# A two-block transformer kernel on one core: short attention pairs, the second down product, the end and the opening in another order

## The reference

```python
# first block: x += mixer(rms_norm(x)); x += conv_ffn(rms_norm(x))
z = h @ w_in                             # pool, q (16 heads of 64), k/v, gates, merge gates
p_c = masked_softmax(q @ k_cmp)          # over compressed keys
imp = sum over heads and overlap of p_c  # importance of each block of 64 keys
_, idx = top_k(imp + forced, 8)          # which 8 blocks each query may see
p_s = masked_softmax(q @ k_sel)          # selected blocks
p_w = masked_softmax(q @ k_win)          # window of 512
o = g0 * p_c @ v_c + g1 * p_s @ v_s + g2 * p_w @ v_w
# second block: x += hybrid_mixer(rmsnorm(x)); x += sqrelu_mlp(rmsnorm(x))
y = square(relu(rmsnorm(x) @ w1)) @ w2   # width 4096; "@ w2" is the second down product
return rmsnorm(x + y)                    # the end
```

## Time and profile before

| what | us |
| --- | --- |
| median of the runs | 2964.59 |
| profiled execution | 2968.41 |
| its span, first to last instruction | 2966.6 |
| TensorE busy | 2901.7 |
| VectorE busy | 2032.5 |
| ScalarE busy | 1447.7 |
| GpSimd busy | 466.8 |

### The profile page before, as it was taken

The page is one execution under the profiler, slowest core; times in us unless marked ns, Lnnn a source line. Parts: engine busy times, 40 slices in busy tenths (PEclk is TensorE's granted clock), DMA queues, the critical chain, the costliest instruction groups (busy, mean ns, idle before and its releaser), DMA issues.

```text
span 2966.6 us, 42764 instructions
## 1 busy us (share of the span) xinstructions
PE 2901.7 (98%) x16282; PEld 2407.7 (81%) x16282; DVE 2032.5 (69%) x3369; ACT 1447.7 (49%) x2448; POOL 466.8 (16%) x764
## 2 busy tenths in 40 slices
PE   9999999899999999999999999999999999999998
PEld 6888888778998887888888888777888788878886
DVE  6653246766775348999989952375655877778888
ACT  4552125887776125445544431275742544444445
POOL 0110004765554120000000000262012000000000
PEclk9999997999999999999999999999999999999999
DMA  4222231000000511333334323001102244474422
GB/s 151 73 84 71 82 117 44 2 1 2 2 2 1 200 56 64 114 114 114 109 133 178 121 86 125 29 2 36 43 29 72 100 166 161 161 302 148 155 100 86
DMA packets 89017, 269.50 MB, mean 91 GB/s; under 512 B 10496, under 2 KB 13696, under 8 KB 88432
## 3 DMA queue, kind: packets, MB, share of 16 engines
q1 hardware_dynamic: 77840, 226.63, 21.5%
q0 software_dynamic: 10976, 40.15, 3.9%
HBM read 190.73 MB, written 70.25 MB: 88 GB/s over the span
## 4 chain that ended last, share of the span: by engine, by line
PE 88%; DVE 4%; ACT 4%; issue 2%; DMA 1%; POOL 0%; SPq 0%; ACTq 0%; DVEq 0%; POOLq 0%
PE PS L256 31%; PE PS L3243 23%; PE PS L3265 15%; PE PS L919 3%; PE PS L933 3%; PE PS L905 2%; PE PS L904 2%; PE PS L1563 1%; PE PS L1598 1%; PE PS L1585 1%; PE PS L956 1%; ACT P_SHORT L1003 1%; PE PS L280 1%; ACT PT L1013 1%; PE PS L947 1%
## 5 line engine op out<-in xcount | busy, mean ns | idle before, releaser
L228 DVE TENSOR_TENSOR WLO<-RAW,WHI 128x1024 fp32r<-128x1024 f32 x94 | 115.7, 1231 | 361.4 <-ACT WHI L223 360.7
L223 ACT CAST WHI<-RAW 128x1024 fp32r<-128x1024 f32 x94 | 98.4, 1048 | 531.2 <-PE PS L256 511.1
L256 PE MATMUL PS<-HLO,WHI 128*128 128x512 f32 x992 | 306.4, 390 | 0.0
L3265 PE MATMUL PS<-DXH,PWH 128*128 128x512 f32 x656 | 256.2, 391 | 3.7 <-DVE DXL L2618 3.7
L3265 PE MATMUL PS<-DXH,PWL 128*128 128x512 f32 x656 | 255.9, 390 | 0.0
L3265 PE MATMUL PS<-DXL,PWH 128*128 128x512 f32 x656 | 255.7, 390 | 0.0
L3243 PE MATMUL PS<-XSH_T,PWH 128*128 128x512 f32 x596 | 233.1, 391 | 5.3 <-DVE PWL L2394 2.4
L3243 PE MATMUL PS<-XSL_T,PWH 128*128 128x512 f32 x596 | 231.9, 389 | 0.0
L3243 PE MATMUL PS<-XSH_T,PWL 128*128 128x512 f32 x596 | 231.9, 389 | 0.0
L256 PEld LDWEIGHTS PS<-HLO,WHI 128*128 128x128 f32 x992 | 186.8, 188 | 39.2
L3243 PE MATMUL PS<-XSH_B,PWL 128*128 128x512 f32 x456 | 177.4, 389 | 0.0
(11 more groups left out here) (444 smaller groups left out, 7160.4 us busy)
## 6 DMA issues: line engine op xcount, KB each, us to landing
W<-in_w SPq DMA_DIRECT2D x61, 1024.0 KB, 6.4
RAW<-in_w SPq DMA_DIRECT2D x96, 512.0 KB, 3.3
hidden<-W SPq DMA_DIRECT2D x54, 512.0 KB, 2.7
DXR<-hidden_t SPq DMA_DIRECT2D x24, 1024.0 KB, 5.3
DXR<-hidden SPq DMA_DIRECT2D x18, 1024.0 KB, 5.1
hidden_t<-W SPq DMA_DIRECT2D x32, 512.0 KB, 3.9
hidden_t<-T SPq DMA_DIRECT2D x16, 512.0 KB, 3.1
X<-in_x SPq DMA_DIRECT2D x8, 512.0 KB, 8.2
```

Of the source, the lines that this page charges most:

```text
L223: nc.scalar.copy(WHI[:, slot, :], RAW[:, slot, :]).then_inc(w_hi, 1)
L228: nc.vector.tensor_tensor(WLO[:, slot, :], RAW[:, slot, :], WHI[:, slot, :].bitcast(F32), ALU.subtract).then_inc(w_lo, 1)
L256: last = nc.tensor.matmul(o[:, half], w[:, slot, cols], x(k)[:, half], start=(k == 0 and w is WHI and x is hi), stop=(done and k == kcs - ...
L3265: last = nc.tensor.matmul(DOWN_BANK(i, p), wt[:, cols], xt[:, k, :], start=(opens and k == 0 and wt is d.pwh(n) and xt is d.xh[r]), stop=( ...
```

## The change

Six places, nothing in what is computed:

- Opening: unit 0 does its last two steps before unit 1 does. VectorE casts the third weight tile and takes its low part before it waits for the reciprocal root; ScalarE leaves that tile out.
- Short pairs, TensorE: up to pair 29, branch 0 of the second head ahead is scored before turn 2, branch 1 after the turns.
- Short pairs, ScalarE: where a pair has more than two turns (pairs 16 to 31), the first exponential of `ahead` comes before copy 2.
- Short pairs, VectorE: all four shifts and the first reciprocal of `ahead` come before CSUM, CMIN and the selection.
- Second down product: the last pair's sums are made beside factor 4 of group 0 instead of factor 0, and SP stores them after block 8 instead of before block 4.
- End: the first mean comes after product 0 and uses bank 0, which product (1, 0) then waits to have read; roots, squares, sums and scalings are in another order.

```diff
--- before.py
+++ after.py
@@ -299,12 +299,14 @@
             for k in range(lead, KC):
                 step(k, 1)
             return
-        for k in range(lead, KC):
-            if k == 6:
-                pe.wait_ge(consts[1], ALL_REST)
-                pe_mean(pe, n)
+        for k in range(lead, KC - 2):
             step(k, 0)
             step(k, 1)
+        pe.wait_ge(consts[1], ALL_REST)
+        pe_mean(pe, n)
+        for b in range(2):
+            for k in range(KC - 2, KC):
+                step(k, b)
 
     def narrow_product(pe, u, hi, lo):
 
@@ -402,7 +404,9 @@
         return N_GATE if i == 2 else P
 
     def act_z1_step(act, u):
-        if u < U_MIX:
+        if 0 < u < U_MIX:
+            if u == 1:
+                act.wait_ge(w_hi, 3)
             act_split(act, u + 2)
         v = u - 1
         if v in ROPE:
@@ -480,8 +484,6 @@
         if U_POOL < u <= U_Q:
             dve.wait_ge(pooled_done, u)
         dve_scaled(dve, 0, u, dst)
-        if u == 0:
-            dve_split(dve, 2)
         if u < U_Q:
             dve_window_sums(dve, u)
         if U_POOL <= u - 1 < U_Q:
@@ -888,11 +890,11 @@
 
         return m + 1 == PAIRS_SHORT
 
-    def pe_scores(pe, n):
+    def pe_scores(pe, n, branches=(0, 1)):
 
         s, qt, g, j = where(n)
         pe.wait_ge(q_lo, s + 1)
-        for branch in range(2):
+        for branch in branches:
             if not short(n):
                 pe.wait_ge(shifted, 2 * n - 1 + branch)
             elif n >= 2:
@@ -985,9 +987,14 @@
             if m in SCORED:
                 pe_cmp_scores(pe, SCORED[m])
             b = batches_of(m)
+            between = ahead and m < PAIRS_SHORT and not waits_for_all(m)
             for i in b[0]:
+                if between and i == 2:
+                    pe_scores(pe, 2 * ahead + 1, (0,))
                 pe_turn(pe, m, i)
-            if ahead and not waits_for_all(m):
+            if between:
+                pe_scores(pe, 2 * ahead + 1, (1,) if len(b[0]) > 2 else (0, 1))
+            elif ahead and not waits_for_all(m):
                 pe_scores(pe, 2 * ahead + 1)
             pe_use(pe, m, b[0])
             if ahead and waits_for_all(m):
@@ -1061,9 +1068,11 @@
             if m >= PAIRS_SHORT:
                 act_out_hi(act, m - 1)
             for i in b[0]:
+                if ahead and len(b) == 1 and i == 2:
+                    act_exp(act, 2 * ahead, 0)
                 act_copy(act, m, i)
             if ahead:
-                if len(b) == 1:
+                if len(b) == 1 and len(b[0]) <= 2:
                     act_exp(act, 2 * ahead, 0)
                 act_exp(act, 2 * ahead, 1)
             if 0 < m < PAIRS_SHORT:
@@ -1231,6 +1240,10 @@
             if ahead:
                 dve_shift(dve, 2 * ahead, 0)
                 dve_shift(dve, 2 * ahead, 1)
+                if m < PAIRS_SHORT:
+                    dve_shift(dve, 2 * ahead + 1, 0)
+                    dve_shift(dve, 2 * ahead + 1, 1)
+                    dve_inverse(dve, 2 * ahead)
             if m >= PAIRS_SHORT:
                 dve_out_lo(dve, m - 1)
             if m in SUMMED:
@@ -1241,7 +1254,7 @@
                 dve_select(dve, SELECTED[m])
             if m >= PAIRS_SHORT and next_seg(m, 1):
                 dve_queries_lo(dve, next_seg(m, 1))
-            if ahead:
+            if ahead and m >= PAIRS_SHORT:
                 dve_shift(dve, 2 * ahead + 1, 0)
                 dve_inverse(dve, 2 * ahead)
                 dve_shift(dve, 2 * ahead + 1, 1)
@@ -2758,13 +2771,13 @@
                     act_end_square(act, m)
                 if (i, p) == (6, 0):
                     break
-        for n in (11, 12, 13):
+        for n in (11, 12):
             act_end_square(act, n)
         act_end_root(act, 0)
-        for n in (14, 15, 16, 17):
+        for n in (13, 14, 15):
             act_end_square(act, n)
         act_end_root(act, 1)
-        for n in (18, 19):
+        for n in (16, 17, 18, 19):
             act_end_square(act, n)
         act_end_root(act, 2)
 
@@ -2918,11 +2931,12 @@
         sp.wait_ge(pw_lo, S2.prods + 4)
         for p in range(4):
             sp_w4(sp, D2, 1, p)
-        sp.wait_ge(t_sums, T_SUMS0 + 4 * FF2_PAIRS)
-        for b in range(2):
-            sp.dma_start(hidden_t[Q_LAST2, b], TSUM[b][:, :]).then_inc(D2.t_out, 16)
         for b in range(4, D2.blocks):
             sp_block(sp, D2, b)
+            if b == 8:
+                sp.wait_ge(t_sums, T_SUMS0 + 4 * FF2_PAIRS)
+                for i in range(2):
+                    sp.dma_start(hidden_t[Q_LAST2, i], TSUM[i][:, :]).then_inc(D2.t_out, 16)
             if b in (10, 17):
                 g = b // 7 + 1
                 sp.wait_ge(pw_lo, S2.prods + 28 * (g - 1))
@@ -2947,7 +2961,7 @@
     END_SQ0, END_SUM0, END_MEAN0, END_ROOT0, END_RSTD0 = 32, 32, 4, 4, 4
     end_prod, end_z, end_quad = job_done, hhi_done, evacuated
     END_PROD0, END_QUAD0, END_Z0 = jobs_before(U_FF2), jobs_before(U_FF2), SPLITS_BEFORE[3] + N_XS
-    END_BANK = (4, 5, 6)
+    END_BANK = (0, 5, 6)
 
     def quad_at(i, p, g=DOWN2_GROUPS - 1):
 
@@ -3025,24 +3039,25 @@
         dve_end_sum(dve, 8)
         dve_end_quad(dve, 0, 1)
         dve_end_sum(dve, 9)
+        dve_end_sum(dve, 10)
         dve_end_quad(dve, 0, 2)
-        dve_end_sum(dve, 10)
-        dve_end_sum(dve, 11)
-        dve_end_quad(dve, 0, 3)
-        dve_end_sum(dve, 12)
         dve_end_ready(dve, 0)
         dve_end_scale(dve, 0, range(0, 1))
+        dve_end_quad(dve, 0, 3)
+        dve_end_sum(dve, 11)
+        dve_end_sum(dve, 12)
+        dve_end_scale(dve, 0, range(1, 3))
         dve_end_quad(dve, 1, 0)
-        dve_end_scale(dve, 0, range(1, 3))
+        dve_end_scale(dve, 0, range(3, 5))
+        dve_end_quad(dve, 1, 1)
+        dve_end_scale(dve, 0, range(5, 6))
         dve_end_sum(dve, 13)
-        dve_end_quad(dve, 1, 1)
-        dve_end_scale(dve, 0, range(3, 5))
+        dve_end_quad(dve, 1, 2)
         dve_end_sum(dve, 14)
-        dve_end_quad(dve, 1, 2)
-        dve_end_scale(dve, 0, range(5, 6))
+        dve_end_scale(dve, 0, range(6, 7))
+        dve_end_quad(dve, 1, 3)
         dve_end_sum(dve, 15)
-        dve_end_quad(dve, 1, 3)
-        dve_end_scale(dve, 0, range(6, KC))
+        dve_end_scale(dve, 0, range(7, KC))
         dve_end_ready(dve, 1)
         dve_end_scale(dve, 1, range(KC))
         dve_end_ready(dve, 2)
@@ -3053,7 +3068,10 @@
         out = bank(END_BANK[i])[:, 0:cols.stop - cols.start]
         pe.wait_ge(end_sum, END_SUM0 + END_SUMMED_IN[i])
         pe.wait_ge(end_sq, END_SQ0 + (8, 16, 20)[i])
-        pe.wait_ge(end_quad, END_QUAD0 + i + 1)
+        if i:
+            pe.wait_ge(end_quad, END_QUAD0 + i + 1)
+        else:
+            pe.wait_ge(D2.quads, quad_at(5, 0))
         last = nc.tensor.matmul(out, ONES[:, :], END_SUM[:, cols], start=True, stop=(i == 0))
         if i:
             last = nc.tensor.matmul(out, ONES[:, :], SQ_LAST[:, cols], start=False, stop=True)
@@ -3066,6 +3084,8 @@
         pe.wait_ge(pw_lo, D2.prod0 + n + 1)
         if b:
             pe.wait_ge(D2.quads, quad_at(5, p))
+            if p == 0:
+                pe.wait_ge(end_root, END_ROOT0 + 1)
         else:
             pe.wait_ge(end_z, END_Z0 + p + 1)
             pe.wait_ge(D2.quads, quad_at(4, p))
@@ -3083,7 +3103,7 @@
         for b in range(2):
             for p in range(4):
                 pe_end_product(pe, b, p)
-                if p == 1:
+                if p == 0:
                     pe_end_mean(pe, b)
         pe_end_mean(pe, 2)
 
@@ -3206,7 +3226,7 @@
                 dve_block_lo(dve, D2, b, p)
             for made in D2.ws_of(g, i, p):
                 dve_dws(dve, D2, *made)
-            if g == 0 and i == 0 and p:
+            if g == 0 and i == 4 and p:
                 dve_t_sums(dve, Q_LAST2, p)
             if (g, i) == (DOWN2_GROUPS - 1, 5):
                 dve_end_z(dve, p)
@@ -3387,6 +3407,10 @@
         for rows in (slice(0, 32), slice(64, 96)):
             last = nc.vector.tensor_scalar(SIN[rows, :], SIN[rows, :], -1.0, None, ALU.mult)
         seq(dve, last)
+        dve.wait_ge(w_loaded[0], 32)
+        dve.wait_ge(job_done, 1)
+        nc.vector.tensor_copy(WHI[:, 0, :], RAW[:, 0, :]).then_inc(w_hi, 1)
+        dve_split(dve, 2)
         dve.wait_ge(rstd_done, 1)
         for u in range(U_POOL, U_MIX):
             dve_z1_step(dve, u)
```

## The result

The changed kernel takes 2971.14 us (median of 20 runs, 2968.11 to 2974.39), the kernel before 2964.88 (20 runs, 2961.39 to 2968.75): ratio 1.0019, 95% interval 1.0013 to 1.0025. It is 6.3 us slower. The forecast was 2962.4 with a range from 2952 to 2971.0, so it was wrong: in sign, and 0.14 us outside the range.

The account below looks back on a forecast made before the run. TensorE is busy 98% of the span, so gains come only where it stands still or runs at its lower clock. Terms: -3.6 - 3.2 - 2.9 + 7.5 = -2.2 us, giving 2962.4 us; range 2952 to 2971.

Parts of the forecast that it names:

- Opening, -3.6: Before the third tile's first product: TensorE restarts 1.92 us sooner and 1.7 of lower clock goes; 3.6 us gained.
- Second down product, -3.2: At its start: the low part comes 1.56 us sooner and 1.6 of work lost to the clock returns; 3.2 gained.
- End, -2.9: Last means and scalings: piece 2 follows piece 1 without a gap and begins 3 us sooner; gain 2.9 us.
- Pair 1, +1.0: Short attention: the sum moves behind ScalarE's exponential, so GpSimd's gated probabilities come 1.0 us later; cost 1.0.
- Pair 31, +3.3: Step to the long pairs: ScalarE's exponential ahead of two copies delays the sum and first long turn; cost 3.3 us.
- Pairs 16 to 30: Short attention: cost 1.0 us at pair 20, against a 1.2 us credit for scores filling waits before turns 2.
- 1.0 here and by the same walk at 8, 1.4 at 4: Pairs 12, 8, 4: selection waits for exponentials, then low parts, so the next pair's first shift is late; these costs in us.
- upper bound of 12: Attention's net cost at most 12 us, with every listed cost half as large again and no credit.
- two signs of being wrong: Wait before the first long turn no longer than before, or pairs 16 to 30 shorter by more than 3 us.
- Rival 1: The attention gains, between -6 and 0 us, as waits before turns go; total 2949 to 2955; chance 0.28.
- Rival 2: Pair 1's longer stall delays the return to full clock by 20 us, losing 8.7 us; total 2971; chance 0.13.
- Rival 3: Opening and down product: stalls shorten but the clock still drops, giving 1.9 + 1.6 only; total 2965.7; chance 0.10.

Follow-up runs that it names:

- k4: Changed kernel with the first head's reciprocal back behind sum, minimum or selection in the short pairs, the four shifts staying ahead: 2958.86 us, 0.9981.
- k5: Changed kernel with VectorE's old order in the short pairs, TensorE's and ScalarE's new order kept: 2954.51 us, 0.9961.
- k10: Changed kernel with the first head's reciprocal back behind sum, minimum or selection and pair 31 old on VectorE and ScalarE: 2954.62 us, 0.9964.
- k2: Kernel before with only the new order of the short attention pairs: 2978.92 us, 1.0051.
- k12: Kernel before with only the end in the new order: 2962.71 us, 0.9991.
- k8: Kernel before with only the last hidden pair's sums and their stores moved in the second down product: 2962.76 us, 0.9991.
- k14: Changed kernel with the first head's reciprocal back behind the selection, only in pairs with a selection (1, 4, 8, ... 28): 2961.53 us, 0.9986.
- k15: Changed kernel with the first head's reciprocal back behind the sum, only in pairs with a sum (1, 3, 7, ... 31): 2969.98 us, 1.0015.
- k3: Changed kernel with pair 31 alone in the old order on VectorE and ScalarE: 2968.64 us, 1.0009.
- k1: Changed kernel with the old order of the short attention pairs on all engines; opening, second down product and end as changed: 2956.48 us, 0.9972.
- k6: Changed kernel with VectorE's old order in pairs with a sum or selection and in pair 31, where ScalarE's is old too: 2955.08 us, 0.9964.
- k13: Changed kernel with the outputs' low parts right behind the reciprocal, ahead of sum, minimum or selection, in the short pairs: 2979.50 us, 1.0043.

## Why the forecast was wrong, step by step

A table of four stretches of the attention, from the profiles. Its marks are the starts of the products with the compressed values (PCT, VCZ) of pairs 0, 4, 16, 31 and 32, each stretch the difference of two starts, in us. In pairs 0 to 15, which have at most two turns, only VectorE's order differs:

| pairs | before | changed | k4 | k5 | k10 |
| --- | --- | --- | --- | --- | --- |
| 0 to 4 | 22.42 | 23.74 | 20.75 | 21.43 | 21.75 |
| 4 to 16 | 56.59 | 64.59 | 56.66 | 56.04 | 56.89 |
| 16 to 31 | 98.57 | 98.77 | 96.21 | 94.76 | 95.88 |
| 31 to 32 | 13.76 | 16.47 | 16.82 | 14.47 | 13.06 |

The changed kernel's stretches are 12.2 us longer in all; the part measured 14.0 (k2), and the profile of the kernel before is of one of its slower executions.

- Opening, -3.6: the mechanism was right (0.82 us stall where 0.8 was worked out, clock kept). TensorE starts again at 37.28, 1.20 us sooner and not 1.92: it was itself 0.7 late before the stall in this execution, so that the stall's length fits is in part luck. -2.2 alone, with an interval that holds 3.6 too.
- Second down product, -3.2: right in kind (1.32 us where about 1.2 was worked out, clock 1.00), -2.0 alone.
- End, -2.9: right, -2.0 alone; in k12's profile the time from the stalled product of the second down product to the last instruction is 308.2 us instead of 311.0, 2.9 less. The three terms were summed to -9.7 and gave -8.4 together; the intervals don't tell the two apart.
- Pair 1, +1.0: it fits these two profiles, both at clock 0.50 there: 2.36 us of wait where 2.1 was worked out, and 1.3 in the table. It is not shown beyond them: with the old order the wait is 1.0 to 2.5 us in other profiles (k12, k8), and with the reciprocal back at pair 1 it is still 2.4 and 2.2 (k14, k15), at other clocks.
- Pair 31, +3.3: right in size, 2.7 in the table and 2.5 in k3 (the stall itself is 4.90, not the 6 named as a sign). But I gave ScalarE's order the lead, and the long stall hangs on VectorE's: with ScalarE's new and VectorE's old order (k5) the stall stays at 3.0 and the stretch takes 14.47, with VectorE's shifts ahead (k4) 16.82. VectorE's new order there with ScalarE's old one was not run.
- Pairs 16 to 30: +0.2 in the table against 1.0 less 1.2 forecast. The credit was not earned by the waits: those before turns fell there from 5.7 to 2.7 us, while the products with the values, which had not waited, waited 3.6 for the same copies. In k5 the two are 2.2 and 0.2.
- **The step that failed** is "1.0 here and by the same walk at 8, 1.4 at 4". It priced pairs 4, 8 and 12 at 3.4, as idle time alone; the table has 8.0 for the stretch, of which TensorE's idle time is 3.8 and its busy time, with the same products at a lower mean clock, 4.2 (windows of the stretch, before and changed):

```profile
504.93:561.52 56.59, 48.97 (x453) 40.90 (x452) 43.50 (x184) 50.92 (x155) 44.78 (x66) 0.98 0.00 1
502.80:567.39 64.59, 53.15 (x454) 45.66 (x453) 43.75 (x180) 51.60 (x157) 45.71 (x70) 0.90 0.01 1
```

The walk failed in two ways. First, I had the low part of the outputs in the queue behind the selection, but followed that queue only to its last item, the next pair's first shift. TensorE waits for the low part itself, since its product with the values two pairs on writes the bank that the low part reads: 0.99, 1.61 and 1.20 us at pairs 5, 9 and 13, 3.8 in all. The wait for the first shift grew by 1.1 on top, not in its place; other waits fell by about 1. TensorE's waits for the shift, in the changed kernel from 505 to 552:

```profile
PE PS L906 <- DVE HMIN L1101: 1.9, 3, 0.8
```

and in the kernel before from 506 to 562:

```profile
PE PS L904 <- DVE HMIN L1092: 0.8, 3, 0.3
```

That the idle time comes near the 3.4 is luck: it is mostly a wait that the walk did not have. Second, a lower clock in these pairs was put at nothing; it is the 4.2. k14 confirms the place: 9.6 us hang on the reciprocal at the selections, priced at 5.4 with pairs 1 and 20.

- The upper bound of 12 was said to be the listed costs half as large again without the credit; that is 13.1 (12 is with the credit). A wait that isn't in the list can't be bounded that way; the part measured 14.0. Neither of the two signs of being wrong that the prediction named came true: both looked at the stall before the first long turn and at pairs 16 to 30, not at 4 to 16.
- Rival 1 was half right: the waits before turns did fall, and k5 and k10 show stretches 16 to 31 shorter by 2.7 to 3.8 us than this profile of the kernel before, by 1.4 to 2.5 than k1's (97.25). VectorE's order gave that back. Rival 2 (2971) has the measured time, by luck and in part by another road: the stretch at half clock from 470 did not grow (34 us in both profiles), the falls came later, at 518 and 528. Rival 3 did not happen: after stalls of 0.82 and 1.32 us the clock stayed up.

The split of the 8.0 us is that of one profile. k2 and k3 have the same order in these pairs; their stretches take 61.3 and 67.2 us, with 11.8 and 12.1 us of idle time (11.4 in the changed kernel, 7.6 before), so the idle time recurs and the clock's part varies by some us. What makes the clock fall is open. Behind stalls of 1.61 and 0.60 us it fell in k3 and stayed at 1.00 in k2, and k6, which has no stall over 1.3 us there, is at the lower level for some 10 us past 504 as well (windows):

```profile
504.00:520.00 16.00, 14.89 (x98) 13.43 (x97) 10.14 (x47) 11.34 (x39) 11.10 (x18) 0.68 0.01 2
520.00:552.00 32.00, 27.50 (x268) 23.18 (x268) 24.05 (x102) 28.43 (x85) 25.23 (x38) 1.00 0.01 2
```

## What to carry to other kernels

On an engine that works in order, an instruction that waits for another engine holds all that is queued behind it, so put it behind the work that is ready, not ahead of it: one reciprocal per short pair cost 11 to 12 us here. When a step is delayed, follow every instruction queued behind it to who waits for it, not only the last one; k13, which cured the wait that showed, made it worse. And leave room in the range for TensorE's clock where new stalls may come: with much the same idle time in pairs 4 to 16, the busy time of the same products was 0.6 to 6.1 us above that of the kernel before in three profiles (k2, changed, k3). When a change is a bundle, time its parts: without VectorE's part (k5) it is 0.4% faster than before, with it 0.2% slower.

## What the runs showed of the hardware that was not expected

The lower clock at the start of the attention begins and ends at times that differ between executions of the same instructions. k8 differs from the kernel before only in the second down product, some 2000 us later. Both have the same wait of TensorE before the first scores, here k8 and then the kernel before:

```profile
472.40 0.30 PE L904 MATMUL PS<-KHD,QS 128*128 128x128 f32 x1 [2.17 <-DVE KF L388]
472.30 0.44 PE L904 MATMUL PS<-KHD,QS 128*128 128x128 f32 x1 [2.16 <-DVE KF L388]
```

Behind it the clock fell at once in the kernel before, and in k8 it stayed up until about 482. Windows of k8:

```profile
469.00:487.00 18.00, 12.32 (x94) 10.73 (x92) 11.27 (x50) 13.21 (x39) 9.97 (x16) 0.91 0.17 59
487.00:504.00 17.00, 15.01 (x90) 13.83 (x90) 10.74 (x53) 10.22 (x36) 12.16 (x20) 0.60 0.00 0
```

The kernel before, same windows (there the lower level goes on to 506):

```profile
469.00:487.00 18.00, 15.72 (x78) 14.28 (x76) 10.39 (x46) 12.02 (x33) 8.51 (x14) 0.59 0.16 59
487.00:504.00 17.00, 15.96 (x90) 14.50 (x89) 10.53 (x55) 10.12 (x36) 12.33 (x21) 0.50 0.01 1
```

The product of pair 0 starts at 479.15 in k8 and at 482.51 in the kernel before, that of pair 4 at 503.00 and 504.93. A single profile can therefore differ by some us from another of the same code; the medians above are what the verdicts rest on.
